# Four RMS norms of a four-layer kernel: sums of squares on all rows instead of in one column

## The reference

```python
def rmsnorm(x, g):
    xf = x.astype(jnp.float32)
    y = xf * lax.rsqrt(jnp.mean(xf * xf, axis=-1, keepdims=True) + EPS)
    return (y * g.astype(jnp.float32)).astype(x.dtype)

def modulate(x, g, shift, scale):
    return rmsnorm(x, g) * (1.0 + scale[:, None, :]) + shift[:, None, :]

# a layer of the first stack; conv_ffn in the second is alike
x = x + g_m[:, None, :] * (mixed @ w_out)
h = modulate(x, norm_ffn, sh_f, sc_f)
x = x + g_f[:, None, :] * swiglu(h, wg, wu, wd)
```

## Time and profile before

| | |
|---|---|
| time, median of 3 runs | 2463.63 us |
| the profiled execution: own time, span | 2464.88, 2463.1 us |
| PE busy | 2390.6 us, 97% |
| DVE, ScalarE (ACT), POOL busy | 1292.0, 951.8, 1097.3 us |
| DMA | 261.54 MB, mean 106 GB/s |
| ACT_TABLE_LOAD at L1238 (the root) | 8, 1283 ns each |

### The profile page before, as it was taken

How to read it: one execution, slowest core, us unless ns; L and a number is a source line. 1 busy time by engine, 2 the same in 40 slices (tenths; PEclk the granted TensorE clock), 3 DMA queues, 4 the chain that set the end, 5 groups by cost and what they waited for, 6 DMA issues and landing times.

```text
span 2463.1 us, 34883 instructions
## 1 busy us (share of the span) xinstructions
PE 2390.6 (97%) x11957; PEld 1935.4 (79%) x11957; DVE 1292.0 (52%) x2318; ACT 951.8 (39%) x1554; POOL 1097.3 (45%) x529
## 2 busy tenths in 40 slices
PE   7989989999999899999999999999999999999998
PEld 6776878888876577888888778888888967888887
DVE  6777564443248753111137976454467464645455
ACT  3458332222335744222244544322246374422222
POOL 2336334444535543444445833444454454344433
PEclk9999999999999899999999999999999999999999
DMA  7531335554322022232332223323233201232222
GB/s 308 194 129 53 129 137 186 190 178 146 102 77 86 18 77 78 94 95 93 102 102 86 73 65 120 103 86 105 92 113 98 95 20 61 86 111 93 96 94 77
DMA packets 64196, 261.54 MB, mean 106 GB/s; under 512 B 7248, under 2 KB 7760, under 8 KB 57936
## 3 DMA queue, kind: packets, MB, share of 16 engines
q1 hardware_dynamic: 61056, 251.00, 30.5%
q10 hardware_dynamic: 3024, 8.98, 1.0%
HBM read 257.86 MB, written 2.10 MB: 106 GB/s over the span
## 4 chain that ended last, share of the span: by engine, by line
PE 88%; DVE 4%; issue 3%; ACT 1%; POOL 1%; DMA 1%; POOLq 1%; DVEq 1%; SPq 0%; ACTq 0%
PE bank L677 26%; PE bank L679 26%; PE bank L678 26%; PE bank L862 3%; PE bank L852 3%; PE bank L881 2%; POOL w_lo L602 1%; DMA first_mods<-in_first 1%; DVE acc L1631 1%; POOLq L666 1%; DVE bank L2259 1%; PE bank L799 1%; PE bank L698 1%; DVE bank L1900 0%; ACT w_hi L1219 0%
## 5 line engine op out<-in xcount | busy, mean ns | idle before, releaser
L602 POOL TENSOR_TENSOR w_lo<-raw,w_hi 128x1024 fp32r<-128x1024 f32 x378 | 917.0, 2434 | 1226.1 <-ACT w_hi L1219 1224.4
L677 PE MATMUL bank<-h_hi,w_hi 128*128 128x512 f32 x1760 | 698.3, 397 | 12.3 <-DVE h_lo L1678 7.8
L679 PE MATMUL bank<-h_hi,w_lo 128*128 128x512 f32 x1760 | 690.2, 392 | 0.0
L678 PE MATMUL bank<-h_lo,w_hi 128*128 128x512 f32 x1760 | 690.0, 392 | 0.0
L1219 ACT ACTIVATE w_hi<-raw 128x1024 fp32r<-128x1024 f32 x378 | 392.5, 1051 | 435.1 <-PE bank L679 432.0
L677 PE MATMUL bank<-g_hi,w_hi 128*128 128x512 f32 x1072 | 418.5, 390 | 0.0
L679 PE MATMUL bank<-g_hi,w_lo 128*128 128x512 f32 x1072 | 417.2, 389 | 0.0
L678 PE MATMUL bank<-g_lo,w_hi 128*128 128x512 f32 x1072 | 417.1, 389 | 0.0
L677 PEld LDWEIGHTS bank<-h_hi,w_hi 128*128 128x128 f32 x1760 | 333.6, 190 | 92.9 <-DVE h_lo L1678 8.7
L679 PEld LDWEIGHTS bank<-h_hi,w_lo 128*128 128x128 f32 x1760 | 333.3, 189 | 71.2
L678 PEld LDWEIGHTS bank<-h_lo,w_hi 128*128 128x128 f32 x1760 | 333.7, 190 | 68.6 <-issue 0.5
(11 more groups left out here) (299 smaller groups left out, 2550.6 us busy)
## 6 DMA issues: line engine op xcount, KB each, us to landing
raw<-in_panels SPq DMA_DIRECT2D x378, 512.0 KB, 3.5
modraw<-in_pairs SPq DMA_DIRECT2D x40, 1024.0 KB, 5.6
first_mods<-in_first SPq DMA_DIRECT2D x4, 2048.0 KB, 22.0
x<-in_x SPq DMA_DIRECT2D x1, 2048.0 KB, 8.1
w<-in_w ACTq DMA_DIRECT2D x1, 2048.0 KB, 8.7
out<-yout ACTq DMA_DIRECT2D x8, 256.0 KB, 2.2
mask<-in_causal ACTq DMA_DIRECT2D x1, 1024.0 KB, 5.0
mask<-in_dilated ACTq DMA_DIRECT2D x1, 1024.0 KB, 6.9
```

Of the source, the lines that this page charges most:

```text
L602: pool.tensor_tensor(w_lo[:, slot, :], raw[:, slot, :], w_hi[:, slot, :].bitcast(F32), ALU.subtract)\
L677: pe.matmul(out, w_h, m_h, start=start, stop=False)
L678: pe.matmul(out, w_h, m_l, start=False, stop=False)
L679: return pe.matmul(out, w_l, m_h, start=False, stop=stop)
```

## The change

In norms 1, 2, 3 and 10 TensorE multiplies a 128x128 tile of ones with acc (512 columns) and then with the last square, both into bank 4 as one accumulation. So the sum of each token stands on all 128 rows at once. ScalarE takes the root of all 512 columns, from bank 4 into acc; DVE takes the reciprocal of acc into bank 5, drains, and goes on with tn. The copy, the addition and the spread are gone, and with them two semaphores and TensorE's wait for the reciprocal. In `project` on ScalarE a root of one column into a new tile, spare, stands before the wait for the last block, so that the table comes there. DVE raises inverse_ready and rstd_ready itself, since later norms count on them.

```diff
-            def rstd(r):
-                column_sums(r)
-                spread(r, bank[5], QB)
+            def sums_on_all_rows(r):
+
+                pe.wait_ge(acc_ready, r - (r > 6))
+                pe.matmul(bank[4][:, :], ones[:, :], acc[:, :], start=True, stop=False)
+                pe.wait_ge(squares_ready, SQ_AT[r] + KB)
+                pe.matmul(bank[4][:, :], ones[:, :], sq[:, (KB - 1) % 2, :], start=False, stop=True).then_inc(sums_ready, 1)
...
-            rstd(1)
+            sums_on_all_rows(1)
             ffn(0, P_FFN0, 1)
-            rstd(2)
+            sums_on_all_rows(2)
...
             def take_root(r, width=D):
-                of = bank[4][:, 0:QB]
-                if r in LAST_BY_PE:
-                    act.wait_ge(eight_ready, LAST_BY_PE.index(r) + 1)
-                    of = root[:, 3 * QB:4 * QB]
-                else:
-                    act.wait_ge(sums_ready, r + 1)
-                act.activation(root[:, 0:QB], of, ACT.Sqrt, bias=EPS, scale=1.0 / width).then_inc(root_ready, 1)
+                act.wait_ge(sums_ready, r + 1)
+                to, of = (acc[:, :], bank[4][:, :]) if r in LAST_BY_PE else (root[:, 0:QB], bank[4][:, 0:QB])
+                act.activation(to, of, ACT.Sqrt, bias=EPS, scale=1.0 / width).then_inc(root_ready, 1)
...
                     if n < KB - 1:
                         split_hi(p0 + n + RING)
+                    if n == KB - 1:
+                        act.activation(spare[:, :], plain[:, 0:1], ACT.Sqrt)
                     act.wait_ge(bank_free, p0 + n + 1)
                     square(r, n, x[:, n, :])
...
             def rstd(r):
-                if r not in LAST_BY_PE:
-                    acc_done()
-                else:
-                    dve.wait_ge(seven_ready, LAST_BY_PE.index(r) + 1)
-                    dve.tensor_copy(root[:, 2 * QB:3 * QB], bank[4][:, 0:QB])
-                    dve.drain()
-                    dve.wait_ge(sums_ready, r + 1)
-                    dve.tensor_tensor(root[:, 3 * QB:4 * QB], bank[6][:, 0:QB], root[:, 2 * QB:3 * QB], ADD)\
-                        .then_inc(eight_ready, 1)
-                invert_root(r)
-                dve.wait_ge(rstd_ready, r + 1)
+                dve.wait_ge(root_ready, r + 1)
+                dve.reciprocal(bank[5][:, :], acc[:, :])
+                dve.drain()
+                dve.sem_inc(inverse_ready, 1)
+                dve.sem_inc(rstd_ready, 1)
```

More of the change, by code:

```diff
@@ L170, in build @@
         plain = sb("plain", [P, 2])
+        spare = sb("spare", [P, 1])
         csil = sb("csil", [P, KB])
@@ L309, in build @@
         scaled_ready = sem("scaled_ready")
-        seven_ready = sem("seven_ready")
-        eight_ready = sem("eight_ready")
         rstd_ready = sem("rstd_ready")
@@ L786, in column_sums @@
                     m = pe.matmul(bank[4][:, j:j + 1], acc[:, P * j:P * j + P], ones[:, 0:1], start=True, stop=True)
-                if r in LAST_BY_PE:
[L788 to L792, removed]
-                m.then_inc(sums_ready, 1)
+                m.then_inc(sums_ready, 1)
+            def sums_on_all_rows(r):
[3 more added lines that the diff above has]
+                pe.matmul(bank[4][:, :], ones[:, :], sq[:, (KB - 1) % 2, :], start=False, stop=True).then_inc(sums_ready, 1)
             def spread(r, to, at):
@@ L1079, in _ @@
             panels(P_OUT1 + 2, KB - 2, h_hi, h_lo)
-            rstd(3)
+            sums_on_all_rows(3)
             ffn(1, P_FFN1, 3)
@@ L1203, in _ @@
             ffn(3, P_FFN3, 9)
-            rstd(10)
+            sums_on_all_rows(10)
         @block.scalar
```

## The result

The changed kernel takes 2472.99 us (median of 6 runs, 2471.68 to 2474.89), the kernel before beside it 2463.86 (6 runs, 2462.25 to 2464.88). The ratio is 1.0038, 95% interval 1.0028 to 1.0049: 9.1 us more, where +2.5 was forecast and the range ended at 2470.2. The profiled execution has a span of 2471.6 us (before 2463.1).

The account below looks back on a forecast made before the run. PE, 88% of the chain that ended last, bounds the kernel. Norms 1, 2, 3 and 10 come 0.34, 0.49, 0.35 and 1.34 us later, clock 0: +2.5 on the median 2463.63 gives 2466.2 us, range 2463.2 to 2470.2.

Parts of the forecast that it names:

- The change touches four places only: Premise: only norms 1, 2, 3 and 10, where TensorE stands for the norm of x, change; together +2.5 us.
- A: Main forecast, 80%: four norms later by +2.5 us in all, 2466.2 us; own range 2463.5 to 2469.
- The reciprocal: DVE, each of the four norms: 512 columns at 6.3 ns a column take 3.37 us, bounds 0.75 to 4.5.
- B: Rival, slower, 5%: each reciprocal column costs 8.5 ns, 4.5 us instead of 3.37 in four norms; 2470.7 us.
- D: Rival, faster, 4%: the reciprocal runs like other DVE instructions, 0.75 us, 2.6 less per norm; 2455.7 us.
- C: Rival, slower, 5%: the reciprocal waits for POOL's w_lo, +1.6 us in each of norms 1 to 3; 2471.0 us.
- Root and table: ScalarE, four norms: root of 512 columns takes 0.60 us; the 1.28 us table load, moved ahead, costs nothing.
- F: Rival, 3%: Square or Copy needs the old table back, so the root reloads its own; +3.5 us, 2469.7.
- the sums on the path: PE, each of the four norms: the second wide product, over the last square, adds 1.05 us including its start.
- Between reciprocal and tn: DVE, each norm: one drain behind the reciprocal, put at 0.10 us until tn (yout in norm 10) starts.
- The clock: Half-clock work after norms 1 to 3: 7.3 us lost now, change from -1.6 to +1.4 us, taken as 0.
- E: Rival, faster, 3%: wide products keep PE's clock up, products after norms 1 to 3 run full; up to -7.3, 2458.9.

Follow-up runs that it names:

- experiments 1: Kernel before plus only an unused one-column tile where the change puts spare, moving everything behind it, g_hi included, by 64 bytes; 2468.42 us, ratio 1.0020.
- experiment 2: The whole change with spare laid behind all other tiles, so that nothing else moves in SBUF; 2468.14 us, ratio 1.0018 to the kernel before.
- experiment 4: Three kernels, the one before with an unused one-column tile in front of g_hi (2468.36 us), all tiles (2462.61), or raw, w_hi and w_lo (2494.19).
- experiment 8: Kernel before with only the root's table loaded ahead, spare behind all other tiles; median 2464.16 us, ratio 0.9991, runs in two groups.
- experiment 6: The change with spare behind all other tiles, a multiplication by 0.1 replacing the reciprocal in the four norms; 2456.11 us, ratio 0.9970 to the kernel before.
- experiment 5: Kernel before with an unused tile of 256 bytes in front of g_hi; 2464.92 us, ratio 0.9999.

## Why the prediction was wrong

- **The step that failed** is "The change touches four places only": a term outside them was put at nothing without a reason. The diff has a line that adds no instruction, the allocation of `spare`, and I priced instructions alone. It moved g_hi by 64 bytes against the weights and cost 4.6 us in products that the change does not touch (experiments 1, 2 and 4). Without it the change runs at 2468.1, 1.9 above the forecast and inside A's own range of 2463.5 to 2469. That the sum could be incomplete by over 3 us outside the four places was written down as a sign to look for, but there was no rival for it.
- **The reciprocal** was right: 3.37 forecast, 3.36 measured in all four. With 32 and 512 columns the slope is (3361 - 354) / 480 = 6.3 ns, as from 4 to 32. B (8.5 ns a column), D (0.75 us) and C (3.36 in norms 1 to 3, beside w_lo, and in norm 10 alike) are out. The Trainium skill's page VectorE: DVE Perf Modes, section "First, the fixed hardware budget", has a repeat count of 8; read as eight cycles a column at its clock, an estimate of 8.3 ns, it does not hold here. Nor does the one result per cycle of its section "Mode 1× (REGULAR) — the baseline".
- **Root and table** were right: 0.60, and no load between sums and root; the load stands at 302.83 us in norm 1, behind the last square but one. F is out. What the load ahead brings to the kernel before by itself is less than it looks (experiment 8).
- **Mis-sized terms**: the sums on the path take 1.12 us, not 1.05; the same product right behind 512-column products takes 1.02 (2456.47), after standing it takes 0.1 more. Between reciprocal and tn there are 0.27 us (0.23 at norm 10), not 0.10, which I had taken from the hand-over behind the spread; they stay at 0.27 when the instruction before takes 0.69 us (experiment 6), so they don't grow with it. That the drain and the signals make them is argued. Together 0.2 a norm: 3.4 instead of 2.5.
- **The clock** was taken as 0, and that holds for the change: 14.7 us of projection work at half clock behind the three norms before, 13.9 after. E is out: the wide sums end at 309.2 and the clock falls at 312.1 in place of 309.1, but TensorE stands until 316.0 and restarts at half clock. Its price was near what half clock costs there (6.6 us in experiment 2, of which fillers brought back 4.2).
- Of the 4.3 us of the change without the move the chains explain 3.4. The interval of its ratio is 2.2 us either way, so the last 0.9 says nothing. That the rest came out inside the range is thus no proof of every term.

## What to carry to other kernels

Read the allocations in a diff as well as the instructions: here a tile of one column shifted the streamed operand against the stationary one, and 3 to 4 ns on 2130 products cost as much as the new norms themselves. New small tiles go behind the large ones, or are padded to 256 bytes, so that the large ones keep their distance as in experiment 5 (the one multiple that ran); the mean ns of untouched product groups in the page shows at once whether that was kept. Before a narrow reciprocal is widened to save a spread, price it by its slope in columns, and where TensorE must stand, look at what the clock does when it restarts.

## What was not expected of the hardware

- The spacing of 512-column products depends on the distance between the streamed tile and the weights. Against the layout of the kernel before: +64 bytes 230.5, 229.8 and 226.7 ns (g_hi with w_hi, g_hi with w_lo, g_lo with w_hi); +128 bytes 232.9 to 233.0 for all; -64 bytes (h, when the weights move) 233.3 to 233.4; +256 and both moved alike 226.7 to 227.0. The next weights are loaded while a tile streams, so two reads of TensorE that meet would explain it; no other engine has to be at work for the cost to be there (experiment 4), but the meeting itself is argued and not shown. The Trainium skill's page SBUF — State Buffer, section "🔬 SBUF: two separate sides", says that TensorE never waits on anyone there. That speaks of other engines, and the trace doesn't contradict it: the cost stands also where they and the DMAs are idle (231.5 against 226.4 ns).
- It can go the other way: with the weights streamed past g (256 columns) the 64 bytes made it 114 ns instead of 120.7.
- The eight small products of the spread take 1.16 us at full clock and 2.08 at half.
- Executions of one program lie up to 9 us apart, and the shorter ones have the higher mean granted clock (experiment 8: 2464.7 us at 0.981, 2455.8 at 0.986).
